# Cutting the loads of transposed table chunks: 32 whole rows to all partitions, or a quarter of every row to 32 partitions

## What is computed

```python
q = (x @ wq).reshape(B, S, PEER_HEADS, PEER_QDIM)              # 8 heads of 256
s1 = einsum('bshd,nd->bshn', q[..., :128], sub1)               # and s2 from the other half with sub2
v1, i1 = top_k(s1, 16); v2, i2 = top_k(s2, 16)
top_s, pos = top_k(v1[..., :, None] + v2[..., None, :], 16)    # idx = i1 * 128 + i2 at pos
wgt = softmax(top_s)
act = gelu(einsum('bphkd,bpd->bphk', u_tab[idx], x))           # u_tab, v_tab: 128 * 128 experts x 1024
out = einsum('bphk,bphkd->bpd', wgt * act, v_tab[idx])
```

## Time and profile before

| | |
|---|---|
| median of three runs | 4635.77 us (4626.92 to 4646.09) |
| the profiled execution's own time | 4643.33 us |
| its span, first to last instruction | 4641.3 us |
| mean granted TensorE clock | 0.98 |
| busy: PE, DVE, POOL, ACT | 94%, 67%, 58%, 39% |
| read from HBM, written | 779.27 MB, 95.42 MB |

### The profile page before, as it was taken

How to read it: one execution, slowest core, us unless ns; L and a number is a source line. 1 busy time by engine, 2 the same in 40 slices (tenths; PEclk the granted TensorE clock), 3 DMA queues, 4 the chain that set the end, 5 groups by cost and what they waited for, 6 DMA issues and landing times.

```text
span 4641.3 us, 73726 instructions
## 1 busy us (share of the span) xinstructions
PE 4355.3 (94%) x21322; PEld 3707.8 (80%) x21322; DVE 3106.7 (67%) x5261; ACT 1803.7 (39%) x3307; POOL 2697.8 (58%) x1489
## 2 busy tenths in 40 slices
PE   7999999999899998999999999989999899999998
PEld 6777876789889997787777778667898889977877
DVE  5665125358889777888866541352689887678888
ACT  3145023124566653333341440231246656533333
POOL 5843753765456675555468438537555556655554
PEclk9999999999999999999999999999999999999999
DMA  3211221234689999999822112112257899989997
GB/s 103 91 55 42 95 68 41 86 86 140 188 260 286 307 319 307 341 347 335 292 83 91 50 46 95 64 41 91 77 159 212 248 283 306 320 308 339 348 341 269
DMA packets 455706, 877.23 MB, mean 189 GB/s; under 512 B 45248, under 2 KB 314048, under 8 KB 452672
## 3 DMA queue, kind: packets, MB, share of 16 engines
q1 hardware_dynamic: 376064, 602.54, 40.7%
q0 software_dynamic: 73728, 268.47, 16.6%
q10 hardware_dynamic: 5696, 3.85, 0.3%
HBM read 779.27 MB, written 95.42 MB: 188 GB/s over the span
## 4 chain that ended last, share of the span: by engine, by line
PE 61%; issue 11%; DVE 10%; DMA 8%; POOL 4%; ACT 3%; SPq 1%; DVEq 0%; ACTq 0%; POOLq 0%; another core or an unknown queue 0%
PE bank L847 6%; PE pair L847 6%; PE bank L1247 5%; PE bank L1252 5%; DMA ring<-v_tab 5%; PE bank L1242 5%; PE bank L1190 4%; PE pair L873 3%; PE pair L849 3%; PE bank L849 3%; PE bank L873 3%; DMA ring<-u_tab 2%; POOL w_lo L684 2%; PE bank L914 2%; PE pair L914 2%
## 5 line engine op out<-in xcount | busy, mean ns | idle before, releaser
L696 POOL TENSOR_TENSOR w_hi<-ring,ones 128x1024 fp32r<-128x1024 f32 x272 | 537.3, 1976 | 745.7 <-PE bank L873 241.8
L684 POOL TENSOR_TENSOR w_lo<-ring,w_hi 128x1024 fp32r<-128x1024 f32 x256 | 615.4, 2404 | 527.7 <-ACT w_hi L1650 520.1
L1190 PE MATMUL bank<-xT,w_hi 128*128 128x384 f32 x2048 | 726.3, 355 | 25.3 <-ACT qk L1666 12.7
L699 POOL TENSOR_TENSOR w_lo<-ring,w_hi 128x1024 fp32r<-128x1024 f32 x272 | 692.0, 2544 | 21.4
L1190 PE MATMUL bank<-xl_peer,w_hi 128*128 128x384 f32 x2048 | 703.3, 343 | 0.0
L1656 ACT CAST w_hi<-ring 128x1024 fp32r<-128x1024 f32 x252 | 265.6, 1054 | 649.4 <-PE bank L1252 444.0
L1650 ACT CAST w_hi<-ring 128x1024 fp32r<-128x1024 f32 x256 | 268.8, 1050 | 590.1 <-DVE ring L2333 424.2
L2430 DVE TENSOR_TENSOR cl<-att,ch 128x384 fp32r<-128x384 f32 x256 | 351.4, 1373 | 146.3 <-ACT ch L1725 143.1
L690 POOL TENSOR_TENSOR w_lo<-ring,w_hi 128x1024 fp32r<-128x1024 f32 x126 | 301.9, 2396 | 249.1 <-ACT w_hi L1656 249.0
L1190 PEld LDWEIGHTS bank<-xT,w_hi 128*128 128x128 f32 x2048 | 402.0, 196 | 29.1 <-ACT w_hi L1650 20.8
L1247 PE MATMUL bank<-w_hi,cl 128*128 128x512 f32 x1524 | 390.6, 392 | 14.2 <-DVE cl L2430 13.9
(11 more groups left out here) (379 smaller groups left out, 9287.2 us busy)
## 6 DMA issues: line engine op xcount, KB each, us to landing
ring<-v_tab SPq DMA_DIRECT2D x252, 512.0 KB
ring<-w_stream SPq DMA_DIRECT2D x240, 512.0 KB
ring<-u_tab SPq DMA_DIRECT2D x512, 128.0 KB
g_spill<-gst SPq DMA_DIRECT2D x240, 192.0 KB
vg<-w_spill SPq DMA_DIRECT2D x64, 704.0 KB
hn<-u_tab SPq DMA_DIRECT2D x256, 128.0 KB
x_last<-u_tab SPq DMA_DIRECT2D x256, 128.0 KB
w_spill<-vg SPq DMA_DIRECT2D x12, 2048.0 KB
```

Source lines behind the costliest of these rows:

```text
L684: nc.gpsimd.tensor_tensor(w_lo[s % 2][:, :], ring[2 + s % 2][:, :], w_hi[s % 2][:, :].bitcast(F32), ALU.subtract)\
L696: nc.gpsimd.tensor_tensor(w_hi[b][:, 0:n], src, ones[:, 0:1].to_broadcast([P, n]), ALU.mult)\
L699: nc.gpsimd.tensor_tensor(w_lo[b][:, 0:n], src, w_hi[b][:, 0:n].bitcast(F32), ALU.subtract)\
L1190: nc.tensor.matmul(out, w_hi[s % 2][:, c * P:(c + 1) * P], dense_parts(c)[part], start=(c == 0 and part == 0), stop=False)
```

## The change

Lines 515 to 528: both places that load a chunk with four DMAs cut it another way. Before, DMA q takes the columns 256q to 256q+255 of all 128 source rows; the source index b (0 to 31) is the partition within a group of 32, and the four row groups lie side by side in the partition. After, DMA k takes the 32 whole rows of row group k (128 KB that lie together in HBM) and spreads them over all 128 partitions: partition 32q+b gets the q-th quarter of row b, in the columns 256k to 256k+255. Where each float lands is the same. The chunk, the number of DMAs, their size and the semaphores are the same too. The new source pattern is written with q outermost (4), then the 32 rows, then 256 floats; the destination pattern is 128 partitions of 256 floats. Behind line 609 a wait is added: SP waits until the two `v_tab` chunks of round 0 of the values have landed before it issues two more that count on the same semaphores.

```diff
--- before.py
+++ after.py
@@ -515,17 +515,17 @@
 
                 for s in range(4):
                     sp.wait_ge(proj_done, slots_done(L, "WQ", i, s - 3))
-                    src = w_stream[L * NSTREAM + (4 * i + (4 * ROUND0["WQ"] + s))].rearrange("(k b) n -> b k n", b=32)
-                    for q in range(4):
-                        sp.dma_start(ring[s][32 * q:32 * q + 32, :].rearrange("b (k n) -> b k n", k=4),
-                                     src[:, :, 256 * q:256 * q + 256]).then_inc(wq_ready[s], 16)
+                    src = w_stream[L * NSTREAM + (4 * i + (4 * ROUND0["WQ"] + s))]
+                    for k in range(4):
+                        sp.dma_start(ring[s][:, 256 * k:256 * k + 256],
+                                     src[32 * k:32 * k + 32, :].rearrange("b (q n) -> q b n", q=4)).then_inc(wq_ready[s], 16)
 
             def load_expert(L, i, s):
 
-                src = u_tab[ds(L * N_KEYS * N_KEYS + 4 * P * i + s * P, P), :].rearrange("(e a) d -> a e d", a=32)
-                for q in range(4):
-                    sp.dma_start(raw[s][32 * q:32 * q + 32, :].rearrange("a (e d) -> a e d", e=4),
-                                 src[:, :, 256 * q:256 * q + 256]).then_inc(u_ready[s], 16)
+                for e in range(4):
+                    src = u_tab[ds(L * N_KEYS * N_KEYS + 4 * P * i + (s * P + 32 * e), 32), :]
+                    sp.dma_start(raw[s][:, 256 * e:256 * e + 256], src.rearrange("a (q d) -> q a d", q=4))\
+                        .then_inc(u_ready[s], 16)
 
             def expert_round(L, i, store=True):
 
@@ -607,6 +607,7 @@
                 load_weights(SPILLED + 1, 1)
                 for s in range(2):
                     sp.wait_ge(split_ready.sem, split_ready.at(L, "UE", ROUNDS["UE"] - 1, s + 3))
+                    sp.wait_ge(w_ready[s], loaded(L, "VE", 0))
                     load_value(L, SPILLED + 1, s)
 
                 sp.wait_ge(proj_done, slots_done(L, "UE", ROUNDS["UE"] - 1, 4))
```

## The result

The changed kernel takes 5232.69 us (median of four runs, 5226.41 to 5238.12) against 4637.19 us (the kernel before, now with a fourth run of 4638.60 us): ratio 1.1287, 95% interval 1.1266 to 1.1307. The profiled execution has a span of 5230.4 us, 589 us more than before. First the page: span, busy time, clock, GB/s by slice, packets, and the chain that ended last.

What follows compares the result with a forecast made beforehand. TensorE, busy for 94% of the span, was taken as the bound, with four full DMA engines binding the score stages after the change: 4641.3 + 816 = 5457 us of span, given as 5450 us, range 5180 to 5850.

Steps and rivals of the forecast that it cites:

- Four shares on four engines: Both changed loads: each DMA is cut into 4 shares, on the same lowest-numbered engines, where 16 took part before.
- 24.1 MB on each: Score stage: each of four engines carries 24.1 MB against 11.4; at 21.5 GB/s 1121 us, +408 us a layer.
- rival 4: Score stages: one engine moves 26.9 GB/s also in 1 KB pieces, +366 us in all, 5000 us; chance 0.05.
- The queue stays full: Score stage: three or four chunks of some 6 us each lie ahead of each u_tab load; every part is bound.
- WQ and the added wait at 0: Query projection (line 520) and the new wait behind line 609: slower landings unseen, wait already met; cost 0 each.
- The clock: Score stages: PE waits 3 to 4 us a chunk, so its clock falls for spells; hidden behind the loads.
- Rival 3: Score stages: TensorE falls to 1.2 GHz and becomes the bound, +554 us a layer, 5740 us; chance 0.08.
- Rivals 1 and 2: Changed loads keep 16 engines: no effect, 4636 us, chance 0.07; or whole rows come quicker (line 527), some 4565 us, 0.03.
- What would show it: Profile signs: small packets 31424, score stage about 163 GB/s at half DMA share, u_tab waits some hundreds of us, PEclk 7 or 8.

Runs made afterwards that it cites:

- late_spill_all: The changed kernel with each 2 MB spill of weights issued behind the loads of slots 0 and 1 of the next round: 5232.90 us, ratio 1.1291.
- eight_dmas: The kernel before with each u_tab chunk loaded by eight DMAs of 64 KB in place of four, still 16 engines each: 4684.20 us, ratio 1.0095.
- wq_only: The kernel before with the new cut only in the query projection (line 520), u_tab loads as before: 4635.01 us, ratio 1.0007.
- wait_only: The kernel before with the added wait alone: 4633.90 us, ratio 0.9994.
- quarter_slots: The kernel before with the new cut for one u_tab chunk in four (slot 0), plus the added wait: 4855.27 us, ratio 1.0480.

## Why the prediction was right, and what was off

It gave 5450 us, and 5180 to 5850; measured is 5233. Step by step:

- *Four shares on four engines*: the count is shown by the packets under 512 B of eight kernels whose DMAs close with 4, 2 or 16 small writes (31424 in the changed kernel, then 43712, 32960, 39104, 42176 twice, 61632 and 94400), each as worked out ahead. That these are always the same engines is not named in a profile; it follows from the plateau of 96 GB/s at a share of 0.27, which successive DMAs don't pass though they overlap in the queue, and from the price of two engines. The Trainium skill (DMA: Bandwidth & Descriptors, on why a DMA increments its semaphore by 16) states both, and the runs agree.
- *24.1 MB on each*: stands. 1009 us for it is **23.9 GB/s; the prediction had 21.5**. That is the term that was mis-sized: +408 us a layer was forecast, +296 came. The upper rate of the range, 24, was nearly the truth. The prediction took a full engine's rate as GB/s over 16 and over the DMA share. By that measure the plateau would be 22.0 (95 GB/s at 0.27), near the 21.5. But four full engines are 0.25 of 16, and the share of 0.27 counts each as busy for 1.08 of the time; so the measure lies low just where an engine is full. It does not explain the whole 17.6 and 18.3 of the 1 KB stages; that the starts and ends of their short bursts do, as the prediction supposed, is not shown. One of its values was not worked out like the rest: 431 GB/s over 16 is 26.9, but over the share of 1.04 too it is 25.9, with which rival 4 would be some 5070 us.
- *The queue stays full*: shown. SP stands in its issues, the four engines run at 23.5 to 24.6 GB/s in every part of the stage, and late_spill_all changed nothing. The prediction had SP's standing there as costing nothing of its own; that holds, as the full engines leave no room for it, and eight_dmas bounds the issues themselves (44 us for twice as many).
- *WQ and the added wait at 0*: shown by wq_only and wait_only.
- *The clock*: in the score stages it is granted at 0.87 (0.96 and 0.97 before), and PE is busy for 727 us in 1009: hidden, as said. Rival 3, TensorE at 1.2 GHz as the bound, would have it busy throughout, so it is excluded.
- *Rivals 1 and 2* (16 engines): excluded by the counts. *Rival 4* (26.9 GB/s, 5000 us): the plateau is 24, so no. The 27 GiB/s per engine that the Trainium skill (DMA: Bandwidth & Descriptors, Specifications) gives, about 29 GB/s, was not reached by 1 KB pieces here.
- *What would show it*: share 0.54 for "about a half", 181 GB/s for 163 (the rate again), the turn's wait 792.6 us for "some hundreds", clock digits 7 and 8, value stage unchanged. The landing in WQ, for which 4 to 8 us was given, can't be read from these profiles.

The prediction priced each score stage by one mean load and one rate. That is right for the changed kernel, where the four engines are full in every part. Carried over to the kernels in between, in the first expectations, it was short by 160 to 295 us, from the upper end of what was expected.

## What to carry to other kernels

Look at the first dimension of both sides of a DMA as it is written, before its size or its contiguity: a small number there (4 column groups ahead of 32 rows) puts the whole transfer on as few engines, and the profile shows it in the count of small packets and in a GB/s row that is flat at a low value while the DMA share looks harmless (0.27 in the projection, 0.54 in the score stage). Price such a cut by the bytes of the fullest engine, part by part of a stage, since a mean over the stage hides the parts that are full already. For the rate, take what such an engine moves when it alone is full (here 24 GB/s) if all loads are cut that way. If only some are, in a stretch where all 16 are busy already, 24 gave no loss for quarter_slots where 8 of 46 chunks were lost; there the rate of that stretch (here 19) came near. A load that moves whole, contiguous rows is no gain in itself: the pieces were 1 KB before and after.

## What was not expected of the hardware

- A DMA cut over 4 engines took SP 549 ns to issue, one over 16 took 317 ns, both in the projection, where no issue is held up for long, and both with 128 pieces of 1 KB.
- One engine moved 24 GB/s in 1 KB pieces when four were busy (96 GB/s in all), but 319 GB/s over 16 engines at a share of 1.03 is 19.9 each. In the value stage 16 engines moved 338 GB/s, 21.1 each, at a share of 0.94. The stages differ in their transfers as well as in the number of busy engines, so which of the two lowers the rate is not shown.
- The same bytes in the same stage cost +223 us for a quarter of the chunks and +287 us for a half: the first quarter of a badly placed load was the dearest here. Why each such chunk costs 2.3 us even away from the spill (147 us over 64 chunks) is not settled.
